# A two-block network in fp32 on one core: 26 of 64 chunks of the later modulation vectors are multiplied and summed on VectorE

## The reference, cut to what matters

```python
c_act = jax.nn.silu(c)                       # [1, 2048]
mod = c_act @ w_ada[l] + b_ada[l]            # [1, 2048] @ [2048, 12288]
sh1, sc1, gt1, sh2, sc2, gt2 = jnp.split(mod[:, None, :], N_MOD, axis=-1)
h = _rmsnorm(x, norm1_g[l]) * (1.0 + sc1) + sh1
...                                          # h @ w_in, RWKV-7 mixer with its scan, pool mixer
x = x + gt1 * mix
h = _rmsnorm(x, norm2_g[l]) * (1.0 + sc2) + sh2
x = x + gt2 * _conv_ffn(h, w_up[l], conv_w[l], conv_b[l], w_down[l])
```

## Time and profile before

| | |
|---|---|
| median of three executions | 2752.37 us (2750.65 to 2770.52) |
| the profiled execution: time | 2762.69 us |
| the profiled execution: span, first to last instruction | 2760.8 us |
| mean granted clock of TensorE in it | 0.979 of full speed |
| busy: TensorE, VectorE, ScalarE, GpSimd | 97%, 64%, 46%, 5% |
| opening of "wkv", with the last of the phase before | 126 to 211.5 us |
| segments 1, 2, 3, 4 | from 211.5, 297, 381, 467 us |

### The profile page before, as it was taken

The page is one execution under the profiler, slowest core; times in us unless marked ns, Lnnn a source line. Parts: engine busy times, 40 slices in busy tenths (PEclk is TensorE's granted clock), DMA queues, the critical chain, the costliest instruction groups (busy, mean ns, idle before and its releaser), DMA issues.

```text
span 2760.8 us, 48190 instructions
## 1 busy us (share of the span) xinstructions
PE 2668.0 (97%) x17744; PEld 2208.3 (80%) x17744; DVE 1765.1 (64%) x2490; ACT 1277.5 (46%) x1767; POOL 145.2 (5%) x149
## 2 busy tenths in 40 slices
PE   5899999999999999999999999999999999999998
PEld 0466667788888888888888888877888888888887
DVE  0454555557777777655576776777587777776554
ACT  1343333445555555444443456633455555554443
POOL 1001110410000000001000000000100000000000
PEclk8799999999999999999999999999999999999999
DMA  9876776254555555555545544444545555555553
GB/s 403 324 308 255 276 288 239 88 188 159 192 185 195 183 195 184 196 211 196 210 169 195 186 153 159 161 161 175 181 168 184 188 189 183 182 185 197 212 198 136
DMA packets 84239, 554.75 MB, mean 201 GB/s; under 512 B 8497, under 2 KB 8625, under 8 KB 19889
## 3 DMA queue, kind: packets, MB, share of 16 engines
q1 hardware_dynamic: 83424, 550.21, 54.4%
q10 hardware_dynamic: 720, 3.21, 0.3%
HBM read 551.29 MB, written 2.10 MB: 200 GB/s over the span
## 4 chain that ended last, share of the span: by engine, by line
PE 82%; issue 9%; DVE 4%; DMA 3%; ACT 1%; POOL 0%; DVEq 0%; SPq 0%; ACTq 0%; POOLq 0%
PE bank L563 37%; PE bank L564 19%; PE banks L563 14%; PE banks L564 7%; DMA raw<-in_stream_dram 3%; PE bank L606 1%; DVE wlo L1593 1%; DVE yb L1609 1%; DVE yb L2214 0%; PE banks L1081 0%; PE banks L1089 0%; PE banks L1100 0%; PE banks L757 0%; POOL bm L2274 0%; DVE ft L2217 0%
## 5 line engine op out<-in xcount | busy, mean ns | idle before, releaser
L563 PE MATMUL bank<-act,whi 128*128 128x512 f32 x3312 | 1190.2, 401 | 2.5 <-DVE x L1957 1.2
L1593 DVE TENSOR_TENSOR wlo<-raw,whi 128x1024 fp32r<-128x1024 f32 x846 | 1033.8, 1232 | 186.2 <-ACT whi L1149 179.0
L1149 ACT ACTIVATE whi<-raw 128x1024 fp32r<-128x1024 f32 x846 | 884.9, 1054 | 400.8 <-PE bank L564 328.8
L564 PE MATMUL bank<-act,wlo 128*128 128x256 f32 x3312 | 930.3, 281 | 0.0
L563 PEld LDWEIGHTS bank<-act,whi 128*128 128x128 f32 x3312 | 623.2, 188 | 170.0 <-issue 19.8
L564 PEld LDWEIGHTS bank<-act,wlo 128*128 128x128 f32 x3312 | 628.1, 190 | 1.9 <-issue 1.7
L563 PE MATMUL banks<-act,whi 128*128 128x512 f32 x1664 | 594.0, 399 | 8.7 <-DVE act L1631 8.7
L563 PE MATMUL bank<-ff,whi 128*128 128x512 f32 x1408 | 493.3, 393 | 1.0 <-DVE wlo L1593 1.0
L564 PE MATMUL banks<-act,wlo 128*128 128x256 f32 x1664 | 470.5, 283 | 0.0
L564 PE MATMUL bank<-ff,wlo 128*128 128x256 f32 x1408 | 392.9, 279 | 0.0
L563 PEld LDWEIGHTS banks<-act,whi 128*128 128x128 f32 x1664 | 316.4, 190 | 84.1 <-issue 9.7
(11 more groups left out here) (250 smaller groups left out, 1574.3 us busy)
## 6 DMA issues: line engine op xcount, KB each, us to landing
raw<-in_stream_dram SPq DMA_DIRECT2D x519, 1024.0 KB, 4.8
x<-in_x_dram SPq DMA_DIRECT2D x1, 2048.0 KB, 14.1
lora_w<-in_lora_dram SPq DMA_DIRECT2D x1, 1536.0 KB, 12.1
pool_w<-in_pool_w_dram ACTq DMA_DIRECT2D x1, 1024.0 KB, 7.1
out_dram<-x SPq DMA_DIRECT2D x2, 512.0 KB, 2.8
out_dram<-x ACTq DMA_DIRECT2D x2, 512.0 KB, 3.0
catt<-in_att_dram ACTq DMA_DIRECT2D x1, 576.0 KB, 3.5
par<-in_params_dram SPq DMA_DIRECT2D x1, 541.5 KB, 3.3
```

Source lines behind the costliest of these rows:

```text
L563: nc.tensor.matmul(tile_bank(t), wh, flat(pair[:, kt]), start=starts and n == 0, stop=False)
L564: mm = nc.tensor.matmul(small_half(t), wl, pair[:, kt, 0], start=False, stop=stops and last)
L1149: nc.scalar.activation(whi[:, k % RING], raw[:, r % RING, 8 * (k % 2):8 * (k % 2) + 8], ACT.Copy)\
L1593: nc.vector.tensor_tensor(wlo[:, k % RING], raw[:, r % RING, 8 * (k % 2):8 * (k % 2) + 8], whi[:, k % RING].bitcast(F32), ALU.subtract).th ...
```

## The change

`SUMMED` names the chunks that leave TensorE: 5, 7, 9, 11 and 13 of vector 2, and 3, 5, 7, 9, 11, 13 and 15 of vectors 3, 4 and 5. For each of these VectorE multiplies the whole chunk (128 x 2048) with silu(c) of its 128 channels, one number per partition, and adds it to `partial(s)`, which is one half of the tile `x` (halves alternate by vector). The first of a vector is a plain multiplication (`tensor_scalar`), the others a multiply-add (`scalar_tensor_tensor`). At slot 15 TensorE multiplies `partial(s)` once with a matrix of ones (`ada_sum`), which adds up its 128 partitions, into the same bank. In the opening the sum of chunk n goes to the head of slot n; in a segment, chunk n + 1 to the head of slot n = 2, 4, 6, 10, 12, 14, and chunk 9 to the head of slot 9. A place of the ring that held a summed chunk is freed by the sum. x is loaded a second time, from ScalarE's queue in slot 1 of segment 4, and VectorE waits for it before the residual.

```diff
--- before.py
+++ after.py
@@ -89,6 +89,26 @@
 LAST_ADA = ADA_PLACE[-1]
 
 RAW = [6 * KT + c for c in range(N_WEIGHT_CHUNKS)]
+
+
+
+
+SUMMED = [(5, 7, 9, 11, 13)] + 3 * [(3, 5, 7, 9, 11, 13, 15)]
+
+
+def summed(a):
+
+    return a % KT in SUMMED[a // KT]
+
+
+def sums_done(a):
+
+    return sum(summed(b) for b in range(a + 1))
+
+
+def products_done(a):
+
+    return ADA0 + a + 1 - sums_done(a) + a // KT
 
 
 def source(r):
@@ -351,6 +371,7 @@
         hi_ready, lo_ready, half_used, tile_sum = sem("hi_ready"), sem("lo_ready"), sem("half_used"), sem("tile_sum")
         token_shifted, tapped, opened, gate_ready = sem("token_shifted"), sem("tapped"), sem("opened"), sem("gate_ready")
         ada_used, ada_copied, ada_turned, mod_ready = sem("ada_used"), sem("ada_copied"), sem("ada_turned"), sem("mod_ready")
+        ada_summed = sem("ada_summed")
         crep_ready, derived = sem("crep_ready"), sem("derived")
         sq_ready, ssq_ready, stat_ready, std_ready = sem("sq_ready"), sem("ssq_ready"), sem("stat_ready"), sem("std_ready")
         normed, ahi_ready, a_ready = sem("normed"), sem("ahi_ready"), sem("a_ready")
@@ -427,6 +448,10 @@
 
             return slice(64 * e, 64 * e + 64)
 
+        def partial(s):
+
+            return flat(x[:, 8 * (s % 2):8 * (s % 2) + 8])
+
         def level_out(level):
 
             return banks4[:, 0:2, 0:256].rearrange("p b (s x) -> p b s x" if level % 2 else "p b (s x) -> p s b x", s=2)
@@ -517,7 +542,12 @@
                 if what == "w":
                     sp.wait_ge(lo_ready, 2 * n + 2)
                 else:
-                    sp.wait_ge(ada_used, (0 if what == "first" else ADA0) + n + 1)
+                    if what == "first":
+                        sp.wait_ge(ada_used, n + 1)
+                    elif summed(n):
+                        sp.wait_ge(ada_summed, sums_done(n))
+                    else:
+                        sp.wait_ge(ada_used, products_done(n))
 
             assert PLACE[FIRST_CHUNK["wout"]] >= LAST_ADA + RING
             load_four("lora")
@@ -594,6 +624,12 @@
                                                 n == 0, n == KT - 1)
                     mm.then_inc(half_used, 1)
 
+            def ada_product(src, column, start, stop):
+                for g in range(4):
+                    mm = nc.tensor.matmul(ada[32 * g:32 * g + 32, :], column, src[:, 512 * g:512 * g + 512],
+                                          start=start, stop=stop, tile_position=(0, 32 * g))
+                mm.then_inc(ada_used, 1)
+
             def ada_chunk(r, n):
 
                 kt = n % KT
@@ -601,11 +637,17 @@
                 if kt == 0 and n // KT:
 
                     pe.wait_ge(ada_copied, n // KT)
-                src = raw[:, r % RING].rearrange("p k n -> p (k n)")
-                for g in range(4):
-                    mm = nc.tensor.matmul(ada[32 * g:32 * g + 32, :], crep[:, kt], src[:, 512 * g:512 * g + 512],
-                                          start=kt == 0, stop=kt == KT - 1, tile_position=(0, 32 * g))
-                mm.then_inc(ada_used, 1)
+                ada_product(raw[:, r % RING].rearrange("p k n -> p (k n)"), crep[:, kt], kt == 0, n < ADA0 and kt == KT - 1)
+
+            def later_chunk(a):
+
+                if not summed(a):
+                    ada_chunk(ADA_PLACE[a], ADA0 + a)
+
+            def ada_sum(s):
+
+                pe.wait_ge(ada_summed, sums_done(KT * s + KT - 1))
+                ada_product(partial(s), ones[:, 0:32], False, True)
 
             def ada_turn(n):
 
@@ -947,7 +989,7 @@
                     mm.then_inc(half_used, 1)
 
             def opening():
-                ada_chunk(ADA_PLACE[0], ADA0)
+                later_chunk(0)
                 for n in range(OPEN_FIRST, 16):
                     full_half("wkv", n, 0, 0, free=n < OPEN_FIRST + 4)
                     for j in LORA_AT.get(n, ()):
@@ -962,7 +1004,9 @@
                     if 6 <= n <= 9:
                         lora_gate(n - 6)
                     for a in (1, 2) if n == OPEN_FIRST else (n,):
-                        ada_chunk(ADA_PLACE[a], ADA0 + a)
+                        later_chunk(a)
+                    if n == 15:
+                        ada_sum(0)
                     if n == 6:
                         kk_step(0)
                     if n == 8:
@@ -994,7 +1038,9 @@
                             quarter(s, q)
                         if part == 1 and n % 2 == 0 and not last:
                             for a in (n, n + 1):
-                                ada_chunk(ADA_PLACE[KT * s + a], ADA0 + KT * s + a)
+                                later_chunk(KT * s + a)
+                        if (n, part) == (15, 1) and not last:
+                            ada_sum(s)
                         next(steps)
                         if n == 10 and part == 0 and not last:
                             kk_spread(s)
@@ -1205,7 +1251,7 @@
 
             def copy_ada(n):
 
-                act.wait_ge(ada_used, KT * (n + 1))
+                act.wait_ge(ada_used, KT * (n + 1) if n < 2 else products_done(KT * (n - 1) - 1) + 1)
                 if n:
 
                     act.wait_ge(ada_turned, n)
@@ -1369,6 +1415,7 @@
                         key_norm(s)
                     if last and n == 1:
 
+                        act.dma_start(x[:], x_in).then_inc(x_loaded, 16)
                         act.dma_start(pool_w[:].rearrange("p g a b n -> p (g a b n)"), pool_w_in).then_inc(pool_loaded, 16)
                         act.dma_start(flat(pool_inv[:]), pool_inv_in).then_inc(pool_loaded, 16)
                     if s and n in (8, 10, 11):
@@ -1890,10 +1937,25 @@
                 token_shift((kraw, rraw, vraw)[m // 2][:, m % 2], FIRST_TILE["wkv"] + wkv_tile(s, m),
                             pcol("mu", 3 + 8 * (m // 2) + m % 2 + 2 * s))
 
+            def sum_chunk(a):
+
+                r, done = ADA_PLACE[a], sums_done(a)
+                src, dst, factor = flat(raw[:, r % RING]), partial(a // KT), crep[:, a % KT, 0:1]
+                dve.wait_ge(raw_full[r % RING], 16 * (r // RING + 1))
+                if a % KT == SUMMED[a // KT][0]:
+                    nc.vector.tensor_scalar(dst, src, factor, None, ALU.mult).then_inc(ada_summed, 1)
+                else:
+                    dve.wait_ge(ada_summed, done - 1)
+                    nc.vector.scalar_tensor_tensor(out=dst, in0=src, scalar=factor, in1=dst, op0=ALU.mult, op1=ALU.add)\
+                        .then_inc(ada_summed, 1)
+
             def segment(s):
                 last = s == SEGMENTS - 1
                 for n in range(0 if s else OPEN_FIRST, 17):
                     h = half_started(s, n) if n < 16 else None
+                    a = n if s == 0 or n == 9 else n + 1
+                    if n < 16 and not last and a % 2 and a < KT and summed(KT * s + a) and (s == 0 or n != 8):
+                        sum_chunk(KT * s + a)
                     if s and n in (8, 11):
                         r_out(s - 1, {8: 1, 11: 3}[n])
                     if h is not None:
@@ -2079,6 +2141,7 @@
                 nc.vector.scalar_tensor_tensor(out=x[:, kt], in0=x[:, kt], scalar=pcol(name, kt), in1=rstd,
                                                op0=ALU.mult, op1=ALU.mult).then_inc(xnew, 1)
 
+            dve.wait_ge(x_loaded, 32)
             residual("wout", 2, True)
             reciprocal_std("x1")
             fill_lo("h2", lambda n: col(gs[:, 1], n), 3, phase="up1")
```

## The result

The changed kernel takes 2770.2 us (median of 20 executions, 2755.7 to 2781.9) against 2754.2 (20 executions, 2745.2 to 2770.5): ratio 1.0044, interval [1.0027, 1.0062]. In a second comparison it took 2770.3 against 2757.6, 1.0036 [1.0011, 1.0061]. The forecast was 2753 us and the range ended at 2766. So the kernel became slower by 0.4%, 7 to 17 us by the interval of the ratio (the two medians lie 16 us apart), where no change was forecast.

A forecast was written before the change was run, and what follows sets the result against it. TensorE's own work was taken as the bound (97% busy), with DMA full at the opening's end. Opening -3.0, segments +3.6, rest 0 gave +0.6 us: 2763.3 profiled, 2753 on the plain-run scale, range 2738 to 2766.

The forecast's parts named there:

- -3.0 (0 to -3.7): Opening: five products leave TensorE and one sum product comes in; transfers start up to 2.8 us earlier; 3.0 us gained.
- the places of the ring: Weight-chunk ring: sums free places within 2 us of TensorE's time, chunk 9's 6 us later but used 14 later; cost 0.
- a sum did wait for its chunk: Changed kernel's trace: a sum having waited for its chunk was named as a sign that the prediction was wrong.
- +3.6 (0.3 to 6.9): Segments 1 to 3 together: 1.2 us later each, though TensorE works 5.6 us less in each.
- D: Slot 2: delay of VectorE's tile reduction by chunk 3's multiplication, reaching TensorE's z step; 2.4 us, bounds 1.3 and 3.5.
- The wait of 3.7 us for tinvt: Level-3 z step: TensorE waits for ScalarE's tinvt copy, 0.33 + 0.93 + 2.4 = 3.7 us.
- Chunk 13's y copy: Slot 12: chunk 13's sum delays the y copy; TensorE's mean step starts at 363.6, not 362.1; 0.93 and 0.5 lost.
- The wait for the wide copy: Slots 8 and 9: removing chunk 9 lengthens TensorE's 1.41 us wait for ScalarE's wide copy to 2.3, gaining nothing.
- chunk 11's us copy: Slot 10: chunk 11's sum moves the copy's end from 350.3 to 351.9; s step waits; 0.5 of 0.93 us kept.
- The 0.65 us of slots 14 to 16: Segment end: chunk 15's sum delays the chain to the masking, awaited by the next segment's first z step, by 0.65 us.
- The falls of the clock: Rival: longer TensorE waits bring more falls, 3.2 us each; three more give 2762, four 2766; chance 0.26.
- The second load of x: Segment 4: 2 MB load takes 5.3 us beside DMA share 0.34; cost 0, up to +2 if a weight chunk came late.

The follow-up runs named there:

- The removal alone: Changed kernel without the sums, 26 chunks' shares missing, their places freed on landing, cut off behind the first residual: 629.7 us, 10.2 below the kernel before cut likewise.
- the short kernel: Cut off behind the first residual, storing x there; here the kernel before with x loaded twice, 641.9 us, against the kernel before, 639.8.
- The best order: Against the kernel before: opening sums 5, 7, 9, 13 behind the cuts, segments only 5, 7 and 11; 636.0 us cut off behind the first residual, full ratio 0.9998.
- the kernel with filler: Changed kernel cut off behind the first residual, plus twelve zero-matrix products in TensorE's waits (slots 2, 8, 12): 655.3 us against 647.0 without them.
- the opening alone: Only the opening's change (chunks 5, 7, 9, 11, 13), segments as before, cut off behind the first residual: 646.8 us, 7.0 above the kernel before cut likewise.
- the short kernel before: The kernel before, cut off behind the first residual, with x stored there and all later phases left out: 639.8 us.

## Why the prediction was wrong

**The opening: the step that failed.** It took the removed 2.8 to 3.7 us as gain, -3.0 (0 to -3.7), and cost the places of the ring at 0, having asked only when the summed chunks' own places come free. Measured is +2.5 (119.8 against 117.2), 5.5 us off and of the other sign; the single pair of before and after would have hidden it (119.8 and 119.2). The removal alone took 113.9, -3.3, as sized, though in that kernel the places also come free earlier. What it missed is the queue behind the new instruction: the sum goes to the head of the slot, the cut that frees a weight chunk's place stands behind it on VectorE, and SyncE waits for that cut. With the order turned round the gain appears (113.3, -3.9). The prediction's own row showed that the DMA engines are full there (0.98), so that a late release is lost at once. The added waits for data (6.6 us against 1.8) also went with more lost clock (9.2 against 6.1). The order within a slot was known; who frees the weight chunks' places, in that order, was not asked. One of the prediction's own signs of being wrong came true here: a sum did wait for its chunk (2.0 us the first, 4.62 us the one at 193.00).

**The segments: the number is near, in good part by luck.** +3.6 (0.3 to 6.9) was forecast without any further fall of the clock, +4.9 measured. But 6.2 us of added lost clock are in the measured figure. Without lost clock the segments take 250.5 us, 1.3 less than those without sums (251.8), or 0.7 more if only the two traces of the kernel before are counted (249.8). So the steps of the sum were too dear by 3 to 5 us, and the clock, which the sum had at nothing, made up for it.

Which steps held? Moving chunk 3 takes 8.0 us off the three segments: 6.2 of waits and 1.9 of lost clock. The waits are 2.1 a segment, where D was 2.4. The multiplication took 2.30 us beside GpSimd, as the 1.477 us of the earlier trace rows had let me expect. The wait of 3.7 us for tinvt came in two pieces, 0.79 us for the zmat copy, which I had not seen behind the reduction, and 2.42 us for tinvt. Chunk 13's y copy is late as worked out. The wait for the wide copy, expected at over 2 us, came as 0.92 us for the us copy ahead of it and 1.14 for wide. Two steps did not come. At slot 10 TensorE was to wait for chunk 11's us copy, and its step at 356.95 started without a wait. The 0.65 us of slots 14 to 16 are absent: from the mean step to the next segment's first z step it was 24.74 us before (363.46 to 388.20) and 24.65 after (368.45 to 393.10).

The Trainium skill (VectorE: DVE Perf Modes, "The perf-mode tier table") has 2293 ns for the two-tensor form; the 22 multiply-adds here took 2387 in the mean. Its 1227 ns for the multiplication agrees with the 1282 measured away from GpSimd. The exclusion of the two engines (the Trainium skill, SBUF — State Buffer, "Who interferes with whom") agrees nearly with the 2301 beside it: GpSimd's instruction ended at 311.87, and 1.28 us behind that is 313.15; the multiplication ended at 312.96.

**The falls of the clock: the rival came in part.** It had a chance of 0.26 and the sum had no term for it, which is the second thing that failed. The segments lost 11.3 us of clock time against 5.1 without sums, nearly two falls more (one was 3.4 in segment 1 of before). The kernel run again shows one at a place that had none, TensorE's row and the windows before and behind it:

```profile
319.28 0.70 PE L799 MATMUL banks<-tinvt,bm 64*64 64x64 f32 x32 [2.36 <-ACT tinvt L1316]
```

```profile
316.00:320.00 4.00, 1.64 (x39) 1.23 (x37) 2.26 (x2) 3.65 (x7) 0.78 (x1) 1.00 0.35 143
320.00:324.00 4.00, 4.00 (x72) 3.27 (x72) 3.39 (x4) 0.22 (x1) 1.25 (x1) 0.57 0.62 236
```

In this trace the added fall follows the added wait. In the first trace of the same kernel the wait of 2.42 us at this place was followed by a granted clock of 1.00 from 320 to 324 us, and a wait of 1.14 us for the wide copy by 0.57 from 349 to 353 us. So the longer waits and the further falls go together in the mean (22.0 us of waits, 11.3 lost, against 7.9 and 5.1), but which wait brings one cannot be told, and that the waits cause the falls is not shown. By the account above, the +4.9 are -16.7 for the products, +14.1 for waits and +6.2 for the clock, which leaves 1.3 without a place.

**The second load of x: 0, as forecast.** 1.0010 [0.9987, 1.0034] in full; 641.9 against 639.8 in the short kernel, from different sets and within the spread of either, so the short pair does not part 0 from its rival's 2 to 4 us. The pooling weight lands in 12.2 us in place of 7.1, and nobody waits for it: its first product comes 59 us after its issue.

**The sum.** In the first 640 us: +2.5 + 4.9 = +7.4, measured +7.2, forecast +0.6. 5.5 of the missing 6.6 us are the opening. The full comparisons say +12 (7 to 17) and +10 (3 to 17); 7 is at their lower end. The stages behind the first residual, the same code in all, took 2118 to 2137 us in seven traces. So whether a few more microseconds are lost there stays open. The best order is faster in its stages, and in full no difference can be measured; its trace reaches the residual's norm at 629.2 us (before: 636.3) and needs 2135.6 behind it (before: 2124.5). I have no cause for that.

## What to carry to other kernels

Before work is put on an engine with room, list what stands behind it in that engine's order, and count releases of buffers among it: a free engine that gives places of a ring free is on the path of the transfers. Where the transfers are the limit, the cheap place for added work is behind the release. One plain multiplication on VectorE was worth moving by a few instructions: the awaited reduction went ahead of it, and it came out from beside GpSimd's (2.30 to 1.28 us). The two effects were not parted. And a forecast of added waits needs a term for the clock, since in the segments here it was larger than the whole difference.

## What was not expected of the hardware

TensorE pauses without waiting for anything that the profile shows, in the middle of a step too. From 126 to 560 us such pauses came to 6.3 us in the kernel with filler, 5.1 with the opening's sums behind the cuts, 3.7 with the opening alone, 0.5 in before and none in the short kernel before. Segments of equal code spread from 253.3 to 258.7 us; between the two ends, both of the kernel before with x loaded twice, 2.1 us are such pauses and 3.4 lost clock. The granted clock fell behind some waits of 1.1 to 1.4 us for the wide copy and not behind others, in kernels with the same order there.
